# Attention heads of 64: values stationary, softmax weights moving and divided ahead of the turn

## The chip, the cores and the metric

The kernel runs on one core of a Trainium2 chip as one launch. The metric is the device time of one execution in microseconds. TensorE (PE in the profile) multiplies, VectorE (DVE) and ScalarE (ACT) work on tiles in SBUF and PSUM, GpSimd (POOL) helps, and SyncE (SP) issues the transfers.

## The reference, cut to what matters

The input is one sequence of 256 tokens with 1024 features. The reference runs two blocks of two layers, ten stages in the kernel: `pa` (pooling and attention), a convolutional feed-forward, a gated linear recurrence, a feed-forward, and then twice a hybrid attention layer (`hy0`, `hy1`), a feed-forward and a small gated embedding. All is fp32. What the change touches is attention:

```
pa:   8 heads of 64, causal, softmax over 256 keys
hy:   difference attention: 4 heads, 2 maps each, values of 128;  a = p[:, 0] - lam * p[:, 1]
      window attention:     8 heads of 64, 2 value heads;  p = e / (sum(e) + exp(sink - m))
      latent attention:     8 heads of 64 (96 in the scores)
      each: out = einsum('bhqk,bkhd->bqhd', p, v); the heads side by side go into a product with weights
```

## The kernel before, in words

Weights come as 241 units of 128x2048 fp32, in the order of use. For each unit SP brings it into one of three `raw` buffers, ACT rounds it to `w_hi` (`split`, L483), DVE forms `w_lo` (L990), and PE multiplies with three products (`three`, L1710 to L1712: high x high, high x low, low x high). A half unit is 24 such matmuls. A buffer of `w_hi` is free again once PE has used the unit three before (`w_used`).

Attention works on maps. A map is the 256x256 matrix of one head, or of one half of a difference head. `pa` has 8 maps. A hybrid layer has 24: maps 0 to 7 of the difference heads (width 128), 8 to 15 of the window heads (64, with a sink), 16 to 23 of the latent heads (64). Each engine has its own loop over maps, written out by hand:

- PE (`attention`, in the block of TensorE): at odd i, `scores(i+1)` computes maps i+1 and i+2 in banks 4 and 5 (L1972, on two halves of the rows at once). Then a filler: half a weight unit of gates. Then `outputs(i-1)` (L2019): per map four matmuls, with the turned softmax weights stationary and the values moving (64 or 128 columns), result by tokens. Then `transposed` for map i (L1991), and for some i also for a pair of finished output tiles, four transposes each.
- DVE (`attention` in the block of VectorE): per odd i it does `logits(i+1)` (L1245 to L1252: distance term, maximum, sink), the evacuation of the filler (L1067), `logits(i+2)`, at i=11 the scaling of the difference outputs, then `outputs` of a group that has ended (L1264 on: reciprocal of the sums, outputs times the reciprocal) and last the split of one weight unit.
- ACT (`attention` in the block of ScalarE): `turn(i-1)` copies the transposed map from its bank into `pt` (L674), `softmax(i)` takes the exponentials with their sums (L693, L695), and at odd i follows the split of a weight unit. For latent maps with odd i `softmax(i)` comes ahead of the turn. Pairs of turned outputs are copied by `turn` as well (L676, L679).

The semaphore `exp_done` releases the transposes of a map, `pt_done` the copy, `pt_ev` the output product, `pv_done` the group on DVE, `o_ev` the transposes of the pair. With a distance term `logits(i)` writes `lg[i % 2]`, so it waits for the transposes of map i-2. In `hy` the product of map 23 stands inside the first product with the branch weights (`onto`, L1710 on), which itself writes the banks that the outputs leave.

## Time and profile before

| | us |
|---|---|
| Median of 3 runs (1570.85 to 1575.32) | 1570.9 |
| The profiled execution | 1571.56 |
| Its span, first to last instruction | 1569.7 |
| PE busy | 1541.5 |
| DVE busy | 1144.7 |
| ACT busy | 910.6 |
| POOL busy | 156.7 |

The span is that of the instructions of the profiled execution; its own time lies 1.9 us above it. Lengths of PE's matmuls overlap, since they are pipelined, so the pace of PE is read from one start to the next and not from the lengths. One fp32 matmul shows as two records (two passes), a product of the kind `three` as one record for each of its three parts. The attention of `pa` lies at about 45 to 90 us, that of `hy0` at 670 to 800, that of `hy1` at 1160 to 1290, and the two hybrid ones repeat each other.

### The profile page before, as it was taken

The numbers are of one execution on the slowest core, as the hardware profiler recorded it, in microseconds if no ns is written. First come the engines' busy times: TensorE is split into PE (matmuls) and PEld (weight loads), VectorE is DVE, ScalarE is ACT, GpSimd is POOL, SyncE is SP. The second block draws the span as 40 slices with busy tenths as digits, with TensorE's granted clock in tenths as the row PEclk, the third lists the DMA queues.
The fourth block names the chain that finished last, engine by engine and source line by source line (L and its number), as shares of the span: only waits on it lengthen the run. The fifth ranks groups of instructions, "written<-read, shape, count | busy, mean of one in ns | idle before, by whom it ended". The sixth has DMA issues, their size and how long they took to land.

```text
span 1569.7 us, 30181 instructions
## 1 busy us (share of the span) xinstructions
PE 1541.5 (98%) x12792; PEld 1494.6 (95%) x12792; DVE 1144.7 (73%) x1382; ACT 910.6 (58%) x1213; POOL 156.7 (10%) x91
## 2 busy tenths in 40 slices
PE   7999999999999999999999999999999999999998
PEld 7899999999999999899899999999889899999998
DVE  6768777888988787778458875678778647776666
ACT  6566544698666565556465644456645555644444
POOL 0211211100011110000030100010000013011010
PEclk9999999999999999999999999999999999999999
DMA  9345555444546545423244555544542334455552
GB/s 317 126 146 184 198 191 181 164 167 150 180 166 214 187 161 200 150 97 119 85 165 162 188 190 185 188 162 162 183 140 91 120 99 160 173 200 202 176 187 77
DMA packets 38412, 258.73 MB, mean 165 GB/s; under 512 B 4768, under 2 KB 5408, under 8 KB 7840
## 3 DMA queue, kind: packets, MB, share of 16 engines
q1 hardware_dynamic: 37872, 255.33, 46.9%
q8 instruction: 83, 1.36, 0.3%
q10 hardware_dynamic: 432, 1.84, 0.3%
q14 instruction: 25, 0.20, 0.0%
HBM read 256.10 MB, written 1.05 MB: 164 GB/s over the span
## 4 chain that ended last, share of the span: by engine, by line
PE 79%; issue 8%; ACT 6%; DVE 5%; POOL 0%; DMA 0%; SPq 0%; POOLq 0%; ACTq 0%; DVEq 0%
PE bank L1710 24%; PE bank L1712 23%; PE bank L1711 23%; PE bank L2019 3%; PE bank L1972 3%; PE bank L1991 2%; ACT w_hi L483 2%; DVE w_lo L990 2%; PE bank L1942 1%; DVE h_lo L1005 1%; PE bank L1915 1%; ACT h_hi L503 1%; DVE qk L1106 1%; DVE x L1081 0%; POOL y_lo L1632 0%
## 5 line engine op out<-in xcount | busy, mean ns | idle before, releaser
L1710 PE MATMUL bank<-h_hi,w_hi 128*128 128x256 f32 x2640 | 751.9, 285 | 14.2 <-DVE h_lo L1005 9.4
L1711 PE MATMUL bank<-h_lo,w_hi 128*128 128x256 f32 x2640 | 742.0, 281 | 0.0
L1712 PE MATMUL bank<-h_hi,w_lo 128*128 128x256 f32 x2640 | 741.8, 281 | 0.0
L990 DVE TENSOR_TENSOR w_lo<-raw,w_hi 128x2048 fp32r<-128x2048 f32 x237 | 549.6, 2322 | 168.6 <-ACT w_hi L483 167.4
L483 ACT ACTIVATE w_hi<-raw 128x2048 fp32r<-128x2048 f32 x237 | 452.8, 1912 | 237.5 <-PE bank L1712 237.5
L1710 PEld LDWEIGHTS bank<-h_hi,w_hi 128*128 128x128 f32 x2640 | 497.7, 189 | 26.6 <-issue 20.9
L1712 PEld LDWEIGHTS bank<-h_hi,w_lo 128*128 128x128 f32 x2640 | 500.9, 190 | 0.0
L1711 PEld LDWEIGHTS bank<-h_lo,w_hi 128*128 128x128 f32 x2640 | 497.3, 188 | 0.3
L1710 PE MATMUL bank<-y_hi,w_hi 128*128 128x256 f32 x1040 | 294.4, 283 | 3.1 <-DVE y_lo L1447 1.4
L1712 PE MATMUL bank<-y_hi,w_lo 128*128 128x256 f32 x1040 | 291.6, 280 | 0.0
L1711 PE MATMUL bank<-y_lo,w_hi 128*128 128x256 f32 x1040 | 291.5, 280 | 0.0
L1710 PEld LDWEIGHTS bank<-y_hi,w_hi 128*128 128x128 f32 x1040 | 195.4, 188 | 6.1 <-ACT sq L641 1.6
L1712 PEld LDWEIGHTS bank<-y_hi,w_lo 128*128 128x128 f32 x1040 | 196.6, 189 | 0.0
L1711 PEld LDWEIGHTS bank<-y_lo,w_hi 128*128 128x128 f32 x1040 | 195.2, 188 | 0.1
L1632 POOL TENSOR_TENSOR y_lo<-qk,y_hi 128x512 fp32r<-128x512 f32 x52 | 109.3, 2101 | 801.4 <-ACT y_hi L602 707.9
L1106 DVE SCALAR_TENSOR_TENSOR qk<-bank,vec,qk 128x255 f32<-128x255 f32 (+1 forms) x264 | 114.9, 477 | 41.1 <-ACT qk L576 32.7
L1056 DVE TENSOR_TENSOR bank<-bank,rinv_t 128x512 f32<-128x512 f32 (+1 forms) x123 | 84.8, 690 | 34.6 <-PE bank L1712 33.7
L576 ACT ACTIVATE qk<-bank,vec 128x256 f32<-128x256 f32 x88 | 44.6, 557 | 104.9 <-DVE bank L1056 104.8
L602 ACT ACTIVATE y_hi<-qk 128x512 fp32r<-128x512 f32 x44 | 27.5, 624 | 62.4 <-PE bank L1712 59.3
L591 ACT ACTIVATE qk<-qk 128x512 f32<-128x512 f32 x44 | 27.8, 633 | 60.3 <-DVE qk L1106 59.9
L674 ACT ACTIVATE pt<-bank 128x512 f32<-128x512 f32 x56 | 33.0, 589 | 48.3 <-PE bank L1991 48.2
L2019 PE MATMUL bank<-val,pt 128*128 128x64 f32 (+1 forms) x448 | 57.0, 270 | 0.7 <-ACT pt L674 0.7
(227 smaller groups left out, 1339.7 us busy)
## 6 DMA issues: line engine op xcount, KB each, us to landing
raw<-W SPq DMA_DIRECT2D x237, 1024.0 KB, 4.8
raw<-W SPq DMA_DIRECT2D x4, 512.0 KB, 7.4
wide<-RW ACTq DMA_DIRECT2D x1, 1280.0 KB, 6.9
x<-XT SPq DMA_DIRECT2D x4, 256.0 KB, 6.6
OUT<-x SPq DMA_DIRECT2D x4, 256.0 KB, 2.0
wide<-CON SPq DMA_DIRECT2D x1, 768.0 KB, 9.7
val<-PE_T ACTq DMA_DIRECT2D x2, 256.0 KB, 2.7
vec<-VEC SPq DMA_DIRECT2D x1, 390.0 KB, 4.6
```

The source lines that it names most:

```text
L483: nc.scalar.activation(w_hi[:, n0 % NW], raw[:, n0 % NRAW], ACT.Copy).then_inc(sems["hi_done"], 1)
L576: ins = nc.scalar.activation(T[:, t], up[:, t * S:(t + 1) * S], ACT.Identity, bias=b, scale=w)
L674: nc.scalar.activation(pt[:, u[1] % 2], src, ACT.Copy).then_inc(sems["pt_ev"], 1)
L990: V.tensor_tensor(w_lo[:, n0 % NW], raw[:, n0 % NRAW], w_hi[:, n0 % NW].bitcast(F32), ALU.subtract)\
L1056: return V.tensor_tensor(z, z, rinv.unsqueeze(1).broadcast_to([P, w // S, S]), ALU.mult)\
L1106: return V.scalar_tensor_tensor(out=dst, in0=src, scalar=w, in1=dst, op0=ALU.mult, op1=ALU.add)
L1632: return G.tensor_tensor(dst, src, hi.bitcast(F32), ALU.subtract)
L1710: T.matmul(out, w[0], a[0], start=start, stop=False, **kw)
L1711: T.matmul(out, w[0], a[1], start=False, stop=False, **kw)
L1712: return T.matmul(out, w[1], a[0], start=False, stop=stop, **kw)
L1972: last = T.matmul(b[:, qt * S:(qt + 1) * S], qk[p:p + w, tq, qt * P:(qt + 1) * P], qk[p:p + w, tk], start=a == 0, stop=a == n - 1)
L2019: last = T.matmul(o, pt[:, i % 2, kt * S + qt * P:kt * S + qt * P + P], value(m["v"], kt), start=kt == 0, stop=kt == 1)
```

## The change

For maps of width 64 (all of `pa`, maps 8 to 23 of a hybrid layer):

- Output product: the values (64 columns) are stationary, and the turned weights move (256 columns). Two heads are done together (`output_pair`), one into partitions 0 to 63 and one into 64 to 127 of their banks, so the result is by features. It is issued at even i for maps i-2 and i-1.
- The result needs no turn. ACT copies it out of its bank (`leave`), at i=17 and i=21, and after the first sigmoid for the last group; in `pa` at i=5 and after the loop.
- The division by the sums can't be done on a result by features. DVE divides the exponentials of each map (`divide`: in `lg`, two multiplies by the reciprocal, ahead of it the sink's add), and `norm_done` releases the transposes instead of `exp_done`.
- The window heads are ordered so that a pair always has one head for each half of the partitions.
- The difference heads (width 128) and the turns of their two pairs stay as they were.

The diff, cut to its core:

```diff
@@ -365,7 +365,8 @@
                                 v=("diff", h), g=h, slot=m, w=128, sink=None, col=2 * h + m))
-            for h in (0, 4, 1, 5, 2, 6, 3, 7):
+            for h in (0, 5, 1, 4, 2, 7, 3, 6):
+
                 p = 64 * (h // 4)
@@ -391,7 +392,7 @@
-        TURNS = {"pa": {5: [0], 8: [1]}, "hy": {12: [0], 13: [1], 16: [2], 17: [3], 21: [4], 24: [5]}}
+        TURNS = {"pa": {}, "hy": {12: [0], 13: [1]}}
@@ -672,11 +678,16 @@
                     nc.scalar.activation(pt[:, u[1] % 2], src, ACT.Copy).then_inc(sems["pt_ev"], 1)
-                elif kind(s) == "hy" and u[1] < 2:
+                else:
                     nc.scalar.activation(ot_tiles(s, u[1]), src, ACT.Copy, scale=v_(f"g_dout{s[-1]}"))\
                         .then_inc(sems["pt_ev"], 1)
-                else:
-                    nc.scalar.activation(ot_tiles(s, u[1]), src, ACT.Copy).then_inc(sems["pt_ev"], 1)
+
+            def leave(s, g):
+
+                gg = total(s, "ogroups") + g
+                act.wait_ge(sems["pv_done"], gg + 1)
+                nc.scalar.activation(ot_tiles(s, g if kind(s) == "pa" else g - 2), bank[2 + gg % 2][:], ACT.Copy)\
+                    .then_inc(sems["o_ev"], 1)
@@ -699,7 +710,10 @@
                 ub = B[s]
-                act.wait_ge(sems["pt_ev"], use_no(s, ("pair", p)) + 1)
+                if p < 2:
+                    act.wait_ge(sems["pt_ev"], use_no(s, ("pair", p)) + 1)
+                else:
+                    act.wait_ge(sems["o_ev"], total(s, "opairs") + p + 1)
                 if p >= 2:
@@ -732,9 +746,14 @@
-                        turn(s, ("pair", 0))
-                        act.wait_ge(sems["pt_ev"], use_no(s, ("pair", 0)) + 1)
+                        leave(s, 0)
+                        act.wait_ge(sems["o_ev"], total(s, "opairs") + 1)
+
+                        act.wait_ge(sems["w_used"], B[s] + 8)
                         to_h(s, hf, 2)
+                    if kind(s) == "hy" and i in (17, 21):
+                        for g in {17: (4, 5), 21: (6,)}[i]:
+                            leave(s, g)
                     held = (9, n - 1) if kind(s) == "hy" else (5,)
@@ -761,6 +780,7 @@
+                leave(s, 1)
                 act.wait_ge(sems["vec_in"], 16)
@@ -770,8 +790,7 @@
                     to_h(s, hf, j)
-                turn(s, ("pair", 1))
-                act.wait_ge(sems["pt_ev"], use_no(s, ("pair", 1)) + 1)
+                act.wait_ge(sems["o_ev"], total(s, "opairs") + 2)
                 to_h(s, hf, 3)
@@ -911,10 +930,10 @@
                     nc.scalar.activation(g, g, ACT.Sigmoid).then_inc(sems["sig_done"], 1)
+                    if b == 0:
+                        leave(s, 7)
                     if b < 2:
                         branch_input(s, b + 2)
-                    if b == 0:
-                        turn(s, ("pair", 5))
                 branch_input(s, 4)
@@ -1252,30 +1271,27 @@
+            def divide(s, i):
+
+                m, a = att_maps(s)[i], 2 + i % 2
+                dve.wait_ge(sems["exp_done"], total(s, "maps") + i + 1)
+                z = sums[:, m["col"]]
+                if m["sink"] is not None:
+                    link(V.tensor_tensor(z, z, esink[:, m["sink"]], ALU.add))
+                link(V.reciprocal(rec[:, a], z))
+                for qt in range(2):
+                    p = lg[:, i % 2, qt * S:(qt + 1) * S]
+                    last = V.tensor_scalar(p, p, rec[:, a, qt:qt + 1], None, ALU.mult)
+                last.then_inc(sems["norm_done"], 1)
+
             def outputs(s, g):
-                K, ms = kind(s), att_maps(s)
+                ms = att_maps(s)
                 mine = sorted((m for m in ms if m["g"] == g), key=lambda m: m["col"])
                 a, n, gg = mine[0]["col"], len(mine), total(s, "ogroups") + g
                 dve.wait_ge(sems["pv_done"], gg + 1)
-                if mine[0]["sink"] is not None:
-                    h = mine[0]["sink"]
-                    link(V.tensor_tensor(sums[:, a:a + n], sums[:, a:a + n], esink[:, h:h + n], ALU.add))
                 link(V.reciprocal(rec[:, 0:n], sums[:, a:a + n]))
                 O = bank[2 + gg % 2]
-                pairs = total(s, "opairs")
-                if K == "pa" or g >= 4:
-                    p = g if K == "pa" else g - 2
-                    if p >= 2:
-
-                        dve.wait_ge(sems["pt_done"], use_no(s, ("pair", p - 2)) + 1)
-                    src = O[:].rearrange("p (q h d) -> p q h d", q=2, h=4)
-                    dst = ot[:, p % 2].rearrange("p (q h d) -> p q h d", q=2, h=4)
-                    for q in range(2):
-                        last = V.tensor_tensor(dst[:, q], src[:, q], rec[:, 0:4, q].unsqueeze(2).broadcast_to([P, 4, 64]),
-                                               ALU.mult)
-                    last.then_inc(sems["o_ev"], 1)
-                    return
                 h, L = g, hys.index(s)
@@ -1303,6 +1319,8 @@
                 logits(s, 1)
+                if kind(s) == "pa":
+                    divide(s, 0)
                 if kind(s) == "hy":
@@ -1318,6 +1336,8 @@
+                    if att_maps(s)[i]["w"] == 64 and att_maps(s)[i]["dist"]:
+                        divide(s, i)
                     if i + 1 < n:
@@ -1328,6 +1348,10 @@
                         logits(s, i + 2)
+                        if att_maps(s)[i + 1]["w"] == 64:
+                            divide(s, i + 1)
+                            if not att_maps(s)[i + 2]["dist"]:
+                                divide(s, i + 2)
                     if kind(s) == "hy" and i == 11:
@@ -1341,7 +1365,7 @@
                     for e in (i - 1, i):
-                        if ended(s, e) is not None:
+                        if ended(s, e) is not None and att_maps(s)[e]["w"] == 128:
                             outputs(s, ended(s, e))
@@ -1981,7 +2005,10 @@
                 if u[0] == "map":
-                    pe.wait_ge(sems["exp_done"], total(s, "maps") + u[1] + 1)
+                    if att_maps(s)[u[1]]["w"] == 64:
+                        pe.wait_ge(sems["norm_done"], normed_no(s, u[1]))
+                    else:
+                        pe.wait_ge(sems["exp_done"], total(s, "maps") + u[1] + 1)
                     src = lg[:, u[1] % 2]
@@ -1995,24 +2022,12 @@
                 m = att_maps(s)[i]
-                g = total(s, "ogroups") + m["g"]
-                if kind(s) == "pa" and i == 0:
-
-                    pe.wait_ge(sems["qk_done"], total(s, "pairs") + 4)
-                if kind(s) == "pa" and i == 4:
-
-                    pe.wait_ge(sems["in_ev"], total(s, "groups") + 7)
-                if kind(s) == "hy" and i == 0:
+                output_bank(s, i)
+                if i == 0:
                     pe.wait_ge(sems["in_ev"], total(s, "groups") + 18)
-                if m["slot"] == 0 and m["g"] >= 2:
-
-                    if kind(s) == "hy" and m["g"] - 2 < 4:
-                        pe.wait_ge(sems["od_free"], 4 * hys.index(s) + m["g"] - 1)
-                    else:
-                        pe.wait_ge(sems["o_ev"], total(s, "opairs") + m["g"] - 2 - 2 + 1)
                 pe.wait_ge(sems["pt_ev"], use_no(s, ("map", i)) + 1)
-                b = bank[2 + g % 2]
+                b = bank[2 + (total(s, "ogroups") + m["g"]) % 2]
                 for qt in range(2):
@@ -2020,6 +2035,37 @@
                     last.then_inc(sems["pv_done"], 1)
+
+            def output_bank(s, i):
+                m = att_maps(s)[i]
+                if m["g"] >= 2 and all(e["g"] != m["g"] for e in att_maps(s)[:i]):
+
+                    if m["g"] - 2 < 4:
+                        pe.wait_ge(sems["od_free"], 4 * hys.index(s) + m["g"] - 1)
+                    else:
+                        pe.wait_ge(sems["o_ev"], total(s, "opairs") + m["g"] - 2 - 2 + 1)
+
+            def output_pair(s, i):
+
+
+                if kind(s) == "pa" and i == 0:
+
+                    pe.wait_ge(sems["qk_done"], total(s, "pairs") + 4)
+                if kind(s) == "pa" and i == 4:
+
+                    pe.wait_ge(sems["in_ev"], total(s, "groups") + 7)
+                output_bank(s, i)
+                output_bank(s, i + 1)
+                pe.wait_ge(sems["pt_ev"], use_no(s, ("map", i + 1)) + 1)
+                for kt in range(2):
+                    for e in (i, i + 1):
+                        m = att_maps(s)[e]
+                        a, r = m["slot"] // 2, 64 * (m["slot"] % 2)
+                        last = T.matmul(bank[2 + (total(s, "ogroups") + m["g"]) % 2][r:r + 64, a * S:(a + 1) * S],
+                                        value(m["v"], kt), pt[:, e % 2, kt * S:(kt + 1) * S],
+                                        start=kt == 0, stop=kt == 1, skip_group_check=True)
+                        if kt and ended(s, e) is not None:
+                            last.then_inc(sems["pv_done"], 1)
@@ -2030,10 +2076,10 @@
                         fill(i)
-                    if kind(s) == "pa" and i == 5:
-                        transposed(s, ("pair", 0))
-                    if i and (kind(s) == "pa" or i < n):
+                    if i and att_maps(s)[i - 1]["w"] == 128:
                         outputs(s, i - 1)
+                    elif i and i % 2 == 0 and (kind(s) == "pa" or i < n):
+                        output_pair(s, i - 2)
                     if kind(s) == "hy" and i == 0:
@@ -2280,10 +2325,9 @@
                             onto(s, b, ub + 25, y_parts(0), True, False, between={
-                                2: lambda: outputs(s, 23),
+                                2: lambda: output_pair(s, 22),
                                 4: lambda: pe.wait_ge(sems["o_ev"], total(s, "opairs") + 5),
                                 6: lambda: pe.wait_ge(sems["o_ev"], total(s, "opairs") + 6)})
-                            transposed(s, ("pair", 5))
                         else:
```

## Rows read from the trace of the kernel before

**Rows 1.** Busy time of each engine, from the page.

```profile
PE 1541.5 (98%) x12792; PEld 1494.6 (95%) x12792; DVE 1144.7 (73%) x1382; ACT 910.6 (58%) x1213; POOL 156.7 (10%) x91
```

**Rows 2.** Busy by stretch: length, then PE, PEld, DVE, ACT, POOL, clock; `hy0`.

```profile
700.00:770.00 70.00, 70.00 (x583) 64.67 (x583) 49.84 (x83) 41.89 (x100) 0.00 (x0) 1.00 0.31 108
```

**Rows 3.** Order of time on PE, maps 8 and 9: start, length, engine, line.

```profile
716.92 0.60 PE L1991 MATMUL bank<-con,lg 128*128 128x128 f32 x4
717.45 1.14 PE L1972 MATMUL bank<-qk 64*128 64x256 f32 x8
718.52 0.39 PE L1710 MATMUL bank<-h_hi,w_hi 128*128 128x256 f32 x1
...
721.47 1.00 PE L2019 MATMUL bank<-val,pt 128*128 128x64 f32 x8
722.30 0.61 PE L1991 MATMUL bank<-con,lg 128*128 128x128 f32 x4
722.67 0.36 PE L1710 MATMUL bank<-h_hi,w_hi 128*128 128x256 f32 x1
```

**Rows 4.** Order of time on PE, a burst on column tiles in `pa`.

```profile
41.40 1.06 PE L1915 MATMUL bank<-sq,con 128*32 128x256 f32 x8
42.39 0.39 PE L1710 MATMUL bank<-w_hi,h_hi 128*128 128x256 f32 x1
```

**Rows 5.** Order of time on PE, map 12 and the turn of pair 0.

```profile
736.01 0.60 PE L1991 MATMUL bank<-con,lg 128*128 128x128 f32 x4
736.45 0.60 PE L1991 MATMUL bank<-con,ot 128*128 128x128 f32 x4
```

**Rows 6.** Order of time on DVE, a multiply in SBUF, and outputs with sink.

```profile
417.92 0.34 DVE L1190 TENSOR_SCALAR geo<-lg,small 128x256 f32<-128x256 f32 x1
...
753.82 0.16 DVE L1263 TENSOR_TENSOR sums<-sums,esink 128x8 f32<-128x8 f32 x1
...
754.25 0.76 DVE L1275 TENSOR_TENSOR ot<-bank,rec 128x256 f32<-128x256 f32 x2
```

**Rows 7.** Order of time on ACT, maps 7 to 9 of `hy0`.

```profile
712.11 1.91 ACT L483 ACTIVATE w_hi<-raw 128x2048 fp32r<-128x2048 f32 x1 [2.59 <-PE bank L1712]
...
715.67 0.19 ACT L695 ACTIVATION_READ_ACCUMULATOR lg<-lg,nm 128x1 f32 x1
717.56 0.60 ACT L674 ACTIVATE pt<-bank 128x512 f32<-128x512 f32 x1 [1.70 <-PE bank L1991]
```

**Rows 8.** Order of time on DVE, difference outputs and the split behind them.

```profile
715.03 0.17 DVE L1264 RECIPROCAL rec<-sums 128x4 f32<-128x4 f32 x1
...
717.78 0.17 DVE L1264 RECIPROCAL rec<-sums 128x4 f32<-128x4 f32 x1
...
720.52 2.28 DVE L990 TENSOR_TENSOR w_lo<-raw,w_hi 128x2048 fp32r<-128x2048 f32 x1
722.72 0.68 DVE L1245 SCALAR_TENSOR_TENSOR lg<-con,bank 128x512 f32<-128x512 f32 x1
```

**Rows 9.** Order of time on ACT, end of the exponentials of map 12.

```profile
734.86 0.19 ACT L695 ACTIVATION_READ_ACCUMULATOR lg<-lg,nm 128x1 f32 x1
```

**Rows 10.** Order of time on ACT and PE, map 22.

```profile
791.10 0.21 ACT L695 ACTIVATION_READ_ACCUMULATOR lg<-bank,nm 128x1 f32 x1
...
791.61 0.61 PE L1991 MATMUL bank<-con,lg 128*128 128x128 f32 x4
```

**Rows 11.** Order of time on PE and ACT, outputs of map 23, first sigmoid.

```profile
797.61 1.00 PE L2019 MATMUL bank<-val,pt 128*128 128x64 f32 x8
...
800.09 1.92 ACT L913 ACTIVATE wide<-wide 128x2048 f32<-128x2048 f32 x1
```

**Rows 12.** Order of time on PE, a gap elsewhere in the kernel.

```profile
401.65 0.70 PE L1780 MATMUL bank<-sq,con 128*128 128x256 f32 x2 [1.85 <-DVE sq L1043]
```

**Rows 13.** PE by stretch behind that gap: length, busy, count, granted clock, DMA.

```profile
402.40:405.70 3.30, 3.30 (x18) 0.50 0.49 149
```

**Rows 14.** Order of time on PE, outputs of map 7 in `pa`.

```profile
84.75 1.10 PE L2019 MATMUL bank<-val,pt 128*128 128x64 f32 x8 [0.69 <-ACT pt L674]
```

More of the change, by code:

```diff
@@ L189, in build @@
             cst_done crms cf_done chi c_ready rope_mm rope_done kro_done
-            s_done lp_done exp_done pt_done pt_ev pv_done o_ev od_free od_ss od_root
+            s_done lp_done exp_done norm_done pt_done pt_ev pv_done o_ev od_free od_ss od_root
             pool_p pm_done psc sig_done bhi b_ready
@@ L309, in build @@
         PLAN = {
-            "pa": dict(groups=8, parts=0, pairs=4, sets=2, maps=8, ogroups=2, opairs=2),
-            "hy": dict(groups=30, parts=5, pairs=13, sets=3, maps=24, ogroups=8, opairs=6)}
+            "pa": dict(groups=8, parts=0, pairs=4, sets=2, maps=8, ogroups=2, opairs=2, turned=0, scaled=8),
+            "hy": dict(groups=30, parts=5, pairs=13, sets=3, maps=24, ogroups=8, opairs=6, turned=2, scaled=16)}
         def total(s, what):
@@ L402, in use_no @@
         def use_no(s, what):
-            n = total(s, "maps") + total(s, "opairs")
+            n = total(s, "maps") + total(s, "turned")
             for i in range(PLAN[kind(s)]["maps"] + 1):
@@ L409, in use_no, with normed_no @@
                     n += 1
+        def normed_no(s, i):
+            if att_maps(s)[i]["w"] == 64:
+                return total(s, "scaled") + sum(m["w"] == 64 for m in att_maps(s)[:i]) + 1
         def ot_tiles(s, p):
@@ L2117, in pa @@
                 onto(s, 0, ub + 8, h_parts(2), True, False, part=(6, 7))
-                transposed(s, ("pair", 1))
                 for n, j in enumerate((0, 1, 3)):
```

## The prediction

> **What bounds the kernel now.** I read the page's busy shares first, to find the engine that sets the end, then the busy time by stretch for one hybrid attention, then the order of time on PE, VectorE (DVE) and ScalarE (ACT). The page gives PE 98% of the span [rows 1]. In the attention of the first hybrid layer PE is busy for the whole 70 us, DVE for 71% and ACT for 60% [rows 2]. So PE work that goes is time won, as long as the other two engines still deliver before PE arrives. DVE and ACT run in order: one late item holds all behind it, whatever their mean share. That is what I look for.
>
> One turn of the loop over maps on PE (odd map i, then i+1) reads in [rows 3]: transposes of map 8 at 716.92, scores at 717.45 (0.53 later), the half unit of weights of map 9 at 718.52, outputs of map 8 at 721.47 (2.95 later), transposes of map 9 at 722.30 (0.84 later), the next half unit at 722.67 (0.37). I call the times of PE "arrivals".
>
> **What PE saves.** Before, the outputs of one head cost 0.84 us although they have 64 columns [rows 3], so 1.68 for two heads. After, a pair is four matmuls of 256 columns with 64 stationary columns each, two side by side. The nearest row is a burst of the same count on tiles of 32 columns: from 41.40 to 42.39, 0.99 us for eight records (four matmuls in two passes) [rows 4]. Going into a tiled burst costs the group ahead 0.53 - 0.37 = 0.16 [rows 3]. So 1.15; I take 1.20, since 64 columns load slower than 32 (lower bound 0.99, upper bound by the scores of the same kind, 1.07 + 0.16 = 1.23, if the tiles do run together). A pair saves 0.48. There are 4 + 8 + 8 = 20 pairs: 9.6 us. The turn of a pair of output tiles goes in 2 + 4 + 4 = 10 places, 0.44 us each (736.01 to 736.45, of the same four transposes) [rows 5]: 4.4 us. The sum is 14.0 us: 2.8 in "pa", 5.6 in each hybrid layer.
>
> The Trainium skill, "TensorEngine Tiling (Array Packing)", section Key Properties, says that a change of tiling mode drains the array. It speaks against this change, which adds one such change in and out per pair. The trace agrees: eight records in 0.99 us plus 0.16 ahead, where records two by two at the spacing of 0.21 would be 0.86. Without that drain the pairs would save 0.82 each, 16.4 in all, rather than 9.6.
>
> **What the division costs DVE.** New per map: a reciprocal of 128x2 and two multiplies of 128x256 from SBUF to SBUF by a column; for windows also the sink's add. The add and reciprocal are 753.82 to 754.25, 0.43; one such multiply takes 0.34 [rows 6], so two in a row are at most 0.68, which gives 1.1 us with a sink and 0.9 without (lower bound 0.8, from two overlapped; upper bound 1.2, with the 0.76 that the old pair of multiplies takes). It is 16 maps a layer, some 16 us of DVE against some 4 removed. DVE goes from 50 to about 62 of 65 to 75 us: it still fits, on the mean. But PE's transposes now wait for it and it stands in DVE's order, so each is a possible stall. Layer by layer, place by place:
>
> - Map 8. The exponentials end at 715.86 [rows 7]; DVE divides to 717.0; PE arrives at 716.92. Stall 0.1.
> - Map 9, the large one. At odd i DVE divides map i as the first thing of its turn of the loop. For i=9 that lies behind everything of turn 7: the difference outputs of groups 2 and 3 (715.03 to 717.78 to 720.52, 2.74 each) and the split of a weight unit (720.52 to 722.72, 2.20) [rows 8]. Those now start after the division of map 8, at 717.0: done at 717.0 + 5.5 + 2.2 = 724.7, map 9 divided at 725.8. PE comes to these transposes after scores and a half unit, with no outputs before them any more: 717.6 + 1.07 + 2.95 = 721.6. Stall 4.2 us. The exponentials of map 9 are no part of it: the turn of map 8 starts at 717.56 [rows 7] and they follow it.
> - Maps 10, 12, 14. ACT's order is split, turn, exponentials; its split waits for the end of the odd half unit (712.11, for the 711.9 of PE) and the exponentials are done 3.75 after it starts [rows 7]. So their end is tied to PE, not to DVE. For map 12 they end at 735.05 [rows 9] and PE arrives at 736.01 [rows 5], 0.96 of slack. PE now arrives 0.48 earlier and the division takes 1.1: 0.48 + 1.1 - 0.96 = 0.6. With what queues behind the late map 9 I take 0.7 each, 2.1 in all.
> - Turn of pair 0 (map 12). The scaling of its tiles on DVE now stands behind the division of map 12: two small ones (0.43) and two multiplies (0.76, both by the [rows 6]), 1.1 to 1.2, less the 0.44 of the transposes of map 12: 0.7.
> - Maps 16, 18, 20: no sink, 0.1 each by the same sum: 0.3.
> - Map 22. Exponentials end at 791.31, PE arrives at 791.61 [rows 10]: slack 0.3. PE now arrives 0.48 + 0.44 earlier, the division adds 0.9, ACT has one copy less ahead (0.5): 0.92 + 0.9 - 0.3 - 0.5 = 1.0.
> - Last pair. Its bank is now emptied by ACT, behind a sigmoid that runs from 800.09 to 802.0 [rows 11], plus a copy of 0.6 [rows 7]: 802.6. Before, DVE did it. PE comes from 797.61 [rows 11] with 1.2 for the pair and 24 matmuls (2.9 at the pace of rows 3): 801.7. Stall 0.9.
>
> That is 0.1 + 4.2 + 2.1 + 0.7 + 0.3 + 1.0 + 0.9 = 9.3 us of stalls against 5.6 saved: each hybrid layer gets 3.7 longer.
>
> **The clock.** After a PE gap of 1.85 us (the matmul at 401.65) the granted clock is 0.50 of 2.4 GHz, so the 1.2 GHz level, over the next 3.3 us, with 18 matmuls where the pace of [rows 3] (24 in 2.95) would fit 27 [rows 12, 13]: about 1.1 us lost. A gap of 4.2 is longer; part of the loss falls into the stall of map 10. I take 0.8 per layer (bounds 0 and 1.7).
>
> The Trainium skill, "TensorE: Matmul & The Clock Gate", section Why this matters for your kernels, warns of idle gaps between bursts for this reason; the trace agrees for one gap, and no row shows one as long as 4 us.
>
> **"pa".** 2.8 saved. Added: a division (0.9) before the very first transposes, and another in the last chain, where PE already waits on the exponentials and their copy (84.75, idle 0.69) [rows 14]; and what follows waits for the split of the rows of h. I let 0.3 of the 2.8 survive (bounds 0 and 2.8).
>
> **The sum.** 2 x (3.7 + 0.8) - 0.3 = +8.7 us. The profiled execution took 1571.56 us (span 1569.7, and 1.9 around it), so 1580.3; it lies 0.7 over the median of the runs, 1570.9. I predict 1580.
>
> **Everything else.** The order of the window heads changes which rows of a bank they write, not the count. On ACT a copy from the bank replaces a copy from the turn. The splits of DVE get late by some 4 us, but their unit is used two turns of the loop (some 20 us) later, and the transfer behind it has more than that. Cover for both: the three weight buffers.
>
> **Rivals.**
> 1. Everything hides: DVE has 20 us free in these 70 [rows 2], so the division costs nothing and 14.0 is won: 1557.6. Against it: the order of DVE around map 9 is written out, and the 4.2 follows from it.
> 2. Only the queue around map 9 stalls (2 x 4.2), the rest is covered by slack: 1571.6 - 14.0 + 8.4 = 1566. For it: the slacks of 0.3 to 1.1 are small numbers, and each of my 0.7s hangs on the 0.48.
> 3. The tiles don't run side by side, so the change doesn't do what it says: 8 passes of 0.21 and 0.2 around them, 1.9 a pair, 0.7 more than I take; where PE would stall anyhow (5 of 8 pairs a layer) it costs nothing. 4 + 3 + 3 pairs: +7, 1587. Against it: the 0.99 of [rows 4] is for 8 records of 256 columns, too short for them one by one.
>
> **Chances.** Forecast 0.64 (1575 to 1586 by the bounds of burst, division and clock); rival 1 0.10; rival 2, or a mix of it with the forecast from 1563 to 1575, 0.18; rival 3 0.08. Within 0.3% (1566.2 to 1575.6; about what a measurement of this kernel can't tell from no change) lies most of rival 2: 0.14. Faster 0.15, slower 0.71. The range 1567 to 1588 leaves out rival 1, a part of rival 2 and a little above.
>
> **What would show it.** Pair bursts of about 1.0 us with two records at each start; PE idle 4 us before the transposes of map 9 in both hybrid layers, with DVE's division as releaser, and a clock of 0.50 behind it; 0.7 before maps 10, 12 and 14; about 1 before the second half of the first branch product, released by ACT's copy. The prediction is wrong if map 9 is not awaited (then rival 1 or 2), or if a pair takes 1.7 or more (rival 3).

## The result, and the profile after

The changed kernel takes 1584.4 us (median of 20 runs, 1573.2 to 1588.2), the kernel before in runs beside it 1573.9 (median of 20, 1570.9 to 1575.3): ratio 1.0061, 95% interval 1.0052 to 1.0070, so 0.6% slower. The profiled execution took 1582.2 us, span 1580.4, against 1571.6 and 1569.7.

Page of the changed kernel, busy time of each engine [rows 1]:

```profile
PE 1532.0 (97%) x12592; PEld 1467.7 (93%) x12592; DVE 1171.4 (74%) x1484; ACT 911.1 (58%) x1213; POOL 155.0 (10%) x91
```

PE has 200 records fewer and 9.5 us less to do; the span is 10.7 longer. So PE waits. Busy by stretch in `hy0`, 70 us of the same attention as in [rows 2], starting 7 us later:

```profile
707.00:777.00 70.00, 63.91 (x495) 55.09 (x496) 54.34 (x116) 39.33 (x94) 0.00 (x0) 0.98 0.29 93
```

PE is busy for 63.9 of 70 us, with 88 records fewer; DVE went from 49.8 to 54.3. The order of time on PE shows where it waits, maps 9 to 14 [rows 3, 5]:

```profile
726.26 1.14 PE L1996 MATMUL bank<-qk 64*128 64x256 f32 x8
...
734.32 0.63 PE L2018 MATMUL bank<-con,lg 128*128 128x128 f32 x4 [3.87 <-DVE lg L1284]
...
739.24 1.08 PE L2064 MATMUL bank<-pt,val 128*64 128x256 f32 x8
740.25 0.66 PE L2018 MATMUL bank<-con,lg 128*128 128x128 f32 x4
...
750.06 0.63 PE L2018 MATMUL bank<-con,lg 128*128 128x128 f32 x4 [0.74 <-DVE lg L1284]
751.17 0.63 PE L2018 MATMUL bank<-con,ot 128*128 128x128 f32 x4 [0.48 <-DVE ot L1364]
...
761.50 0.63 PE L2018 MATMUL bank<-con,lg 128*128 128x128 f32 x4 [0.89 <-DVE lg L1284]
```

A pair (line L2064, 739.24 to 740.25) takes 1.01 us for eight records, and in the trace they start two by two, 0.01 us apart: the tiles run side by side. Map 9 is awaited 3.87 us, and its releaser is the division (L1284). From the scores of map 10 (the L1996 row) to the transposes of map 12 it is 23.80 us; before, 717.45 to 736.01, 18.56 [rows 3, 5]. DVE's own order says why [rows 8]:

```profile
724.94 0.62 DVE L1284 TENSOR_SCALAR lg<-lg,rec 128x256 f32<-128x256 f32 x2
725.48 0.17 DVE L1293 RECIPROCAL rec<-sums 128x4 f32<-128x4 f32 x1
...
728.23 0.17 DVE L1293 RECIPROCAL rec<-sums 128x4 f32<-128x4 f32 x1
...
730.97 2.28 DVE L1009 TENSOR_TENSOR w_lo<-raw,w_hi 128x2048 fp32r<-128x2048 f32 x1
733.17 0.15 DVE L1280 TENSOR_TENSOR sums<-sums,esink 128x2 f32<-128x2 f32 x1
...
733.56 0.62 DVE L1284 TENSOR_SCALAR lg<-lg,rec 128x256 f32<-128x256 f32 x2
```

Map 8 is divided, then come the outputs of groups 2 and 3 and the split, and only then map 9. Behind the gap the clock stands at its lower level, 1.2 of 2.4 GHz [rows 13] (all engines: PE, PEld, DVE, ACT, POOL, then the granted clock):

```profile
735.10:738.40 3.30, 3.30 (x17) 3.30 (x17) 2.73 (x7) 3.27 (x9) 0.00 (x0) 0.50 0.68 283
```

What this costs can be read from the rows: from the transposes of map 9 (734.32) over half a weight unit to the pair (739.24) it is 4.92 us; before, the same work took 0.37 + 2.95 = 3.32 [rows 3]. So the low clock costs 1.6 us.

At the end of the stage, order of time on PE, then ACT [rows 10, 11]:

```profile
803.19 1.08 PE L2064 MATMUL bank<-pt,val 128*64 128x256 f32 x8 [0.39 <-ACT pt L680]
805.18 0.63 PE L2018 MATMUL bank<-con,lg 128*128 128x128 f32 x4 [0.91 <-DVE lg L1284]
...
809.47 0.36 PE L1734 MATMUL bank<-y_hi,w_hi 128*128 128x256 f32 x1 [0.39 <-issue]
...
814.65 0.57 ACT L689 ACTIVATE qk<-bank 128x512 f32<-128x512 f32 x1
```

In "pa", order of time on PE:

```profile
52.23 0.66 PE L2018 MATMUL bank<-con,lg 128*128 128x128 f32 x4 [0.82 <-DVE lg L1284]
...
62.39 0.63 PE L2018 MATMUL bank<-con,lg 128*128 128x128 f32 x4 [1.11 <-DVE lg L1284]
...
77.88 0.35 PE L1734 MATMUL bank<-h_hi,w_hi 128*128 128x256 f32 x1 [1.12 <-DVE wide L1086]
...
85.76 0.63 PE L2018 MATMUL bank<-con,lg 128*128 128x128 f32 x4 [1.78 <-DVE lg L1284]
```

The transposes of maps 0, 2 and 7 wait for their divisions, 3.7 us in all (map 4 another 0.17). Before, none of them waited, the place of the 1.12 had 0.84, and the 0.69 ahead of the last product stands in both kernels.

The table below gives stage lengths in every trace: the time between the same two matmuls of weight units, counted from the first, so that kernels can be laid beside each other. "pa" is up to the 481st, `hy0` from the 5041st to the 5761st, `hy1` from the 8641st to the 9121st, which ends ahead of the last pair; the loops are the three looped feed-forward stretches (720, 1680 and 1800 matmuls). "10 to 12" is the time from the scores of map 10 to the transposes of map 12 in `hy0`.

```
kernel                     pa    hy0    hy1    loops              10 to 12
before                     85.9  141.3  102.3  83.2 201.4 215.6   18.56
changed                    90.9  146.4  107.3  85.2 197.2 211.4   23.80
no_division                83.9  137.6   98.0  85.2 197.2 211.4   18.01
division_alone             90.4  149.4  110.4  85.2 201.4 215.6   23.48
pairs_hybrid               85.9  146.4  107.2  85.2 197.2 215.7   23.78
pairs_latent               85.4  142.5  103.3  85.2 201.4 211.4
pairs_latent_inputs_late   86.4  141.2  102.0  85.2 201.4 215.6
pairs_latent_scaled_first  86.3  140.0  100.8  85.2 201.4 215.6
nine_early                 86.9  147.9  108.8  85.2 201.4 215.6   25.21
nine_early_split_late      87.4  143.3  104.1  85.2 201.4 215.6   20.64
root_late                  87.1  147.6  105.3  85.2 201.4 215.6   23.38
pool_left_out              85.7  147.3  107.1  85.2 201.4 211.4
before_again               86.1  141.3  102.3  85.2 201.4 215.6
changed_again              89.9  146.4  107.3  83.2 201.4 215.6
```

So by stage the change costs 5.0 in "pa", 5.1 in `hy0` and 5.0 in `hy1`; the loops, whose code it doesn't touch, gave 6.4 back in this one execution, and 1.6 went in a stretch ahead of `hy0` where the clock was low.

The profiled execution is not a typical one. The mean granted clock of the 20 runs lies between 0.993 and 0.997, in 13 of them at 0.996 or more; the profiled one has 0.993, the lowest value. As an estimate, 0.993 means 2 x 0.007 x 1580 = 22 us at the lower level and 0.996 means 13. The stretches behind map 9 take 6.8 of these in both layers together and the end of the kernel 2.3, so in most runs there was hardly room for the 6.8 us of low clock that this trace shows in "pa" (below). The loss of 5.0 there overstates what most runs lose.

### The profile page after: what moved, and what is told of

It is laid out like the page before. It is cut to its first block, busy times and chain, and to the rows that moved or that the text cites. A ratio compares the mean times of both kernels' runs of the same rounds, so it can differ in the third digit from the quotient of the medians.

```text
span 1580.4 us, 29864 instructions
## 1 busy us (share of the span) xinstructions
PE 1532.0 (97%) x12592; PEld 1467.7 (93%) x12592; DVE 1171.4 (74%) x1484; ACT 911.1 (58%) x1213; POOL 155.0 (10%) x91
## 4 chain that ended last, share of the span: by engine, by line
PE 74%; ACT 9%; issue 9%; DVE 7%; POOL 0%; DMA 0%; ACTq 0%; SPq 0%; POOLq 0%; DVEq 0%
PE bank L1734 23%; PE bank L1736 22%; PE bank L1735 22%; ACT w_hi L489 3%; PE bank L1996 2%; DVE w_lo L1009 2%; PE bank L2018 1%; ACT lg L706 1%; PE bank L2064 1%; PE bank L2034 1%; DVE h_lo L1024 1%; DVE lg L1284 1%; PE bank L1939 1%; PE bank L1966 1%; ACT h_hi L509 1%
## 5 line engine op out<-in xcount | busy, mean ns | idle before, releaser
L608 ACT ACTIVATE y_hi<-qk 128x512 fp32r<-128x512 f32 x44 | 27.4, 624 | 59.7 <-PE bank L1736 54.3
L1656 POOL TENSOR_TENSOR y_lo<-hf,y_hi 128x512 fp32r<-128x512 f32 x8 | 16.7, 2098 | 369.7 <-ACT y_hi L721 369.7
```

What stands on the lines that cost most here:

```text
L1656: return G.tensor_tensor(dst, src, hi.bitcast(F32), ALU.subtract)
```

## The experiments

### The saving alone and the division alone

`no_division` leaves out DVE's division (outputs are not normalised); `division_alone` is the kernel before with the division added, so values are divided twice.

```diff
  # no_division
-                 divide(s, ...)                  (all four places)
-                     pe.wait_ge(sems["norm_done"], normed_no(s, u[1]))
+                     pe.wait_ge(sems["exp_done"], total(s, "maps") + u[1] + 1)
  # division_alone: before, and the same places and waits added
+                 divide(s, ...)
+                     pe.wait_ge(sems["norm_done"], normed_no(s, u[1]))
```

> The changed kernel without the division: VectorE's add of the sink, reciprocal and multiplies by the reciprocals are left out, and TensorE's transposes wait for the exponentials (so the outputs of these heads are not normalised). If TensorE's part of the change is worth what I counted and the stalls come from the division: 14.0 us saved over 20 pairs and 10 turns, some 2 given back at the ends: 0.992 of before, about 1561 us; no gap over 0.5 us before the transposes of map 9. If the pairs save little: 0.998 to 1.0. If something other than the division makes the changed kernel longer: above 1.0.

> The kernel before with the division added at the places where the changed kernel has it, the old product, scaling and turns kept (values are divided twice, so outputs are not the reference's). If the division's places in VectorE's order cost what I worked out: map 9 waits 3.5 us and loses 1 to the clock, map 22 0.6, the turn of pair 0 0.7, in each hybrid layer, and the first stage some 4 (it lost 4.3 in the changed kernel in spite of 2.8 saved, so up to 7): +15 to +20 us, ratio 1.010 to 1.013. If the division hides: below 1.002.

`no_division`: 0.9934 (0.9913 to 0.9955), 1562.6 us. `division_alone`: 1.0121 (1.0096 to 1.0146), 1594.9 us. Both ratios are as expected. The stages show 10.0 us saved without the division (2.0 + 3.7 + 4.3), and 4.5 + 8.1 + 8.1 = 20.7 lost by the division alone. The price of one pair can be read from a turn of the loop over latent maps, from one group of scores to the next, first in the kernel before, then without the division:

```profile
769.75 2.60 PE L1972 MATMUL bank<-qk 64*128 64x256 f32 x16
780.74 2.60 PE L1972 MATMUL bank<-qk 64*128 64x256 f32 x16
```

```profile
756.39 2.60 PE L1988 MATMUL bank<-qk 64*128 64x256 f32 x16
766.86 2.60 PE L1988 MATMUL bank<-qk 64*128 64x256 f32 x16
```

10.99 and 10.47: a pair saves 0.52 (I had taken 0.48). With 0.44 for each turn that would be 14.8 over the kernel; a third of it is lost even with no division. The idle time of PE that is new in its three attention stages adds up to 3.4 us of that: PE now comes early to other things. The rest was not placed. One of the new waits, in `hy0`:

```profile
726.42 0.63 PE L2008 MATMUL bank<-con,lg 128*128 128x128 f32 x4 [0.51 <-ACT lg L706]
```

### Which stage pays

`pairs_hybrid` has "pa" as before; `pairs_latent` has "pa" and the window maps as before.

```diff
+ PAIRED = ("mla", "win")        # pairs_latent: ("mla",)
- if att_maps(s)[i]["w"] == 64:  (division, waits, order of the maps, emptying of the banks)
+ if att_maps(s)[i]["v"][0] in PAIRED:
```

> The changed kernel with the first attention stage (8 causal maps) as before; window and latent maps of both hybrid layers by pairs. If the first stage costs 4 us of the change's 9 to 10: 1.003 of before and no displacement up to 100 us of the span. If the first stage is neutral, as I predicted (-0.3): 1.006, as the changed kernel.

> Only the 8 latent maps of each hybrid layer by pairs, all else as before. Saved per layer 4 pairs x 0.48 and 2 turns x 0.44 = 2.8; stalls 3 x 0.17 and 1.5 at map 22: -0.8 a layer, -1.6 us in all, ratio 0.999. If the division of these maps, which have no sink and stand late in VectorE's order, hid altogether: -5.6 us, 0.9965. If they stalled like the window maps (0.7 to 1 each): +2, 1.001.

`pairs_hybrid`: 1.0042 (1.0025 to 1.0059), "pa" 85.9 as before, both hybrid stages as in the changed kernel: so "pa" has its own share of the loss (1.0042 against 1.0061), and my forecast for it was wrong. `pairs_latent`: 0.9996 (0.9978 to 1.0014), which can't be told from 0.999 or from no change. By stage it was 1.2 and 1.0 longer than before, where I had expected 0.8 shorter. Two stalls at map 22 were the known ones; one was new (order of time on PE):

```profile
761.91 0.63 PE L2060 MATMUL bank<-con,ot 128*128 128x128 f32 x4 [1.00 <-DVE ot L1332]
```

The turn of pair 2 waits for the scaling of its tiles, which DVE now does behind the divisions of maps 16 and 17.

### GpSimd beside the division

`pool_left_out` is the changed kernel without the pooling branch's arithmetic on GpSimd (POOL).

```diff
-                     link(G.tensor_tensor(nxt[...], cur[...], cur[...], ALU.add))
-                         link(G.tensor_tensor(r, r, pa_con[...], ALU.mult))
-                         last = G.tensor_tensor(pool_u[...], r, pool_u[...], ALU.subtract)
+                     last = G.tensor_tensor(pool_u[:, g, 8:12], ...)     (4 columns)
```

> The changed kernel with GpSimd's adds and multiplies of the pooling branch in the first stage left out (the pooling branch is then not computed). If VectorE's multiplies of the division, up to 1.2 us instead of 0.35, are long because GpSimd works in SBUF at the same time, and the end of the stage waits for GpSimd: no multiply over 0.4 us there, the stage ends 3 us earlier than in the changed kernel (2 behind before instead of 5), 1.004. If they are long for another reason: they stay, the stage ends at most 1 us earlier, 1.006.

In the changed kernel, order of time on DVE and POOL in "pa":

```profile
60.71 1.53 DVE L1284 TENSOR_SCALAR lg<-lg,rec 128x256 f32<-128x256 f32 x2
62.16 2.81 DVE L1009 TENSOR_TENSOR w_lo<-raw,w_hi 128x2048 fp32r<-128x2048 f32 x1
...
70.83 0.62 DVE L1284 TENSOR_SCALAR lg<-lg,rec 128x256 f32<-128x256 f32 x2
...
79.20 1.86 DVE L1284 TENSOR_SCALAR lg<-lg,rec 128x256 f32<-128x256 f32 x2
...
84.39 1.22 DVE L1284 TENSOR_SCALAR lg<-lg,rec 128x256 f32<-128x256 f32 x2
```

```profile
62.05 0.77 POOL L1688 TENSOR_TENSOR wide<-wide 128x256 f32<-128x256 f32 x1
62.90 2.67 POOL L1689 TENSOR_TENSOR wide<-wide 128x256 f32<-128x256 f32 x1
77.14 6.73 POOL L1684 TENSOR_TENSOR wide<-wide 128x512 f32<-128x512 f32 x4 [11.57 <-DVE wide L1086]
```

The same two multiplies take 0.62 when POOL is idle and 0.90 to 1.86 (four of the eight pairs) when it works. Nor is it DVE alone that waits: DVE's split at 80.99 kept its 2.28 us, and POOL's last add, begun at 81.00, took 2.87 us, where the same add at 59.87 took 0.61:

```profile
81.00 2.87 POOL L1684 TENSOR_TENSOR wide<-wide 128x256 f32<-128x256 f32 x1
```

With POOL's work left out:

```profile
59.54 0.61 DVE L1284 TENSOR_SCALAR lg<-lg,rec 128x256 f32<-128x256 f32 x2
...
77.13 0.62 DVE L1284 TENSOR_SCALAR lg<-lg,rec 128x256 f32<-128x256 f32 x2
...
82.34 0.61 DVE L1284 TENSOR_SCALAR lg<-lg,rec 128x256 f32<-128x256 f32 x2
```

All eight pairs are at 0.61 or 0.62, and "pa" is 85.7 us long, not 90.9. Order of time on PE, maps 2 and 7:

```profile
60.30 0.63 PE L2010 MATMUL bank<-con,lg 128*128 128x128 f32 x4 [0.19 <-DVE lg L1284]
...
83.10 0.63 PE L2010 MATMUL bank<-con,lg 128*128 128x128 f32 x4 [1.18 <-DVE lg L1284]
```

The wait for map 2 fell from 1.11 to 0.19 and that for map 7 from 1.78 to 1.18, 1.5 us together. Three later kernels with the changed kernel's "pa" (`nine_early`, `nine_early_split_late`, `root_late`) split the loss: there the clock stayed at 1.00 and "pa" took 86.9 to 87.4. So about 1.4 us (87.1 - 85.7) is the contention with POOL, in line with the 1.5 of the two waits and half of the 3 that I had expected, and the other 3 to 4 are a low clock, which the changed kernel's trace shows as the last figures but two of this stretch of PE (length, busy, clock):

```profile
86.50:93.30 6.80, 6.22 (x20) 0.50 0.13 55
```

A low clock came here in both executions of the changed kernel (6.8 us of it in the first, about half in the second) and in `division_alone`, not in those three, though PE's gaps ahead were the same (1.78 and 0.69 us in the changed kernel, 1.77 and 0.69 in `nine_early`). What decides it stays open. The whole time of `pool_left_out`, 1.0065 (1.0041 to 1.0090), shows nothing of the gain: its trace has one loop at the longer 201.4 and lost 3.1 us to a low clock ahead of `hy0`. By the whole time alone this experiment is inconclusive; the verdict rests on the rows.

The Trainium skill, "SBUF — State Buffer", section SBUF: two separate sides, says that VectorE and GpSimd share a pair of ports, given to one of them for a whole instruction. The rows agree for the multiplies from SBUF to SBUF (0.90 to 1.86 for 0.62) and for POOL's add beside the split (2.87 for 0.61). I did not weigh it in the prediction.

### The order of DVE around map 9

```diff
  # nine_early: divide(9) between the outputs of groups 2 and 3
-                         divide(s, i)            (first of turn 9)
                              outputs(s, ended(s, e))
+                             if e == 6:
+                                 divide(s, 9)
  # nine_early_split_late: and the split of turn 7 behind divide(10)
-                         after(fillers[7][0])    (end of turn 7)
                              divide(s, i + 1)
+                             if i == 9: after(fillers[7][0])
  # root_late: and ScalarE's square root two maps later
-                     if kind(s) == "hy" and i == 9:
+                     if kind(s) == "hy" and i == 11:
```

> The changed kernel with VectorE's division of map 9 between the outputs of groups 2 and 3, not behind both and a split. By my theory the gap of 4.2 us before map 9 goes (divided at 729.4 in the time of the changed kernel's trace, TensorE there at 730.2) and most of it comes back one map later, for the logits of map 10 start no earlier than before: a gap of 3 to 4 us before the transposes of map 10; 1 us a layer gained: 1.005 of before. By the rival (only the place of map 9's division costs): 4 to 5 us a layer, 1.000.

> The same, and the split of the weight unit (2.2 us) moved from behind the outputs of group 3 to behind the division of map 10. By my theory map 10 then waits about 2.3 us and map 11 about 1: 2.2 to 3.2 us a layer gained against the changed kernel: 1.002 to 1.003 of before. By the rival, everything gained already by the place of map 9: 1.000, as the kernel beside it.

> As nine_early_split_late, and ScalarE's square root of the difference norms (it waits for the outputs of group 3, and the copy of the turned map 9 stands behind it) moved two maps later. If that copy alone held the pair of maps 8 and 9 (2.55 us in the kernel without this move): the gap before the pair goes and 2 us a layer are gained, 1.002 of before. If VectorE is the limit there, which is what I expect from its order (map 10 is divided at 731.8 in that trace, whatever ScalarE does): the gap moves to the transposes of map 10, at most 0.5 us a layer gained, 1.004 to 1.005.

`nine_early`: 1.0092 (1.0072 to 1.0112); `nine_early_split_late`: 1.0049 (1.0033 to 1.0065); `root_late`: 1.0070 (1.0057 to 1.0084). Order of time on PE in `nine_early`, map 10, and its clock behind it:

```profile
733.48 1.08 PE L2020 MATMUL bank<-con,lg 128*128 128x128 f32 x4 [4.38 <-DVE lg L1284]
```

```profile
733.50:740.00 6.50, 6.50 (x31) 0.56 0.45 159
```

Map 9 is not awaited any more, map 10 is, for 4.38 us: DVE starts its logits no earlier than before. That is my theory's sign, but not its price: I expected 1 us a layer gained, and 1.5 was lost, for the low clock lasted longer than behind the gap of 3.87 (0.50 from 732.3 to 739.1, against 3.4 us). With the split moved as well, order of time on PE, then by stretch:

```profile
731.95 0.63 PE L2022 MATMUL bank<-con,lg 128*128 128x128 f32 x4 [2.17 <-DVE lg L1284]
737.28 0.63 PE L2022 MATMUL bank<-con,lg 128*128 128x128 f32 x4 [0.59 <-DVE lg L1284]
```

```profile
732.00:737.50 5.50, 4.91 (x38) 1.00 0.45 147
```

2.17 at map 10 and 0.59 at map 11 (2.3 and 1 expected), no loss of clock, and both stages 3.1 to 3.2 shorter than in the changed kernel. The whole time shows less of it: 1.0049, where I had 1.002 to 1.003. The profiled run is again a favourable one, with a mean clock of 0.998; 7 of the 12 runs have 0.994 to 0.996, so their clock fell for longer, where isn't known.

`root_late` answers a question that I had put wrongly: the gap stood before the transposes of map 10 all along, not before the pair. It stayed there (2.19), as it must if DVE is the limit; but the moved square root has its own table, the exponentials' table is loaded again ahead of map 12 (1.28 us at 740.00), and a gap of 2.16 came there (1.38 in `hy1`). Order of time on PE in `hy0`, and its clock behind both gaps:

```profile
731.22 0.63 PE L2022 MATMUL bank<-con,lg 128*128 128x128 f32 x4 [2.19 <-DVE lg L1284]
...
743.94 0.63 PE L2022 MATMUL bank<-con,lg 128*128 128x128 f32 x4 [2.16 <-DVE lg L1284]
```

```profile
732.50:735.70 3.20, 3.20 (x15) 0.50 0.46 97
746.20:749.40 3.20, 3.20 (x16) 0.50 0.27 38
```

Here the clock fell behind gaps as long as the one behind which it had stayed at 1.00. That makes `hy0` 4.3 us longer than in `nine_early_split_late`; `hy1`, where the clock held, is 1.2 longer. So the move costs some 1.2 us a layer, and most of the 4.3 is clock.

### A version that might beat both

```diff
  # pairs_latent_inputs_late: pairs_latent, and on ScalarE
-                     if kind(s) == "hy" and i == n - 2:   (ahead of softmax(22))
+                     if kind(s) == "hy" and i == n - 1:   (behind softmax(23))
                          branch_input(s, 0)
                          branch_input(s, 1)
  # pairs_latent_scaled_first: and on VectorE
+                         if kind(s) == "hy" and i == 15:
+                             outputs(s, 4)
                          if by_pair(s, i + 1):
                              divide(s, i + 1)
```

> Only the latent maps by pairs, and ScalarE's two copies of the first branch inputs (2 x 0.52 us) moved from ahead of the exponentials of map 22 to behind those of map 23. If the gap of 1.3 to 1.5 us at map 22 comes from ScalarE's order: it falls to 0.5 or less, 1 us a layer, so -2 to -4 us against before, ratio 0.998. If that gap comes from VectorE (the divisions of maps 22 and 23 one behind the other): it stays, ratio 0.9996 as without the move. If the first branch product then waits for its inputs: above 1.000.

> As pairs_latent_inputs_late, and VectorE scales the outputs of window group 4 ahead of the divisions of maps 16 and 17, not behind them. The gap of 1.2 us before the turn of pair 2 falls to 0.5 or less, 0.8 us a layer: 0.998 of before (between 0.997 and 0.999). If the divisions behind it now make map 16 wait instead: no gain, 0.999.

0.9990 (0.9979 to 1.0001) and 0.9991 (0.9982 to 1.0001). The first move took 1.3 us off each layer against `pairs_latent` and both gaps at map 22 are gone; since `pairs_latent` had been 1 us a layer behind the kernel before, that makes 0.1 and 0.3 us against before, not the 1 to 2 of my 0.998. The second took another 1.2; the turn of pair 2 starts at once:

```profile
761.95 0.60 PE L2061 MATMUL bank<-con,ot 128*128 128x128 f32 x4
```

By stage this version is 2.8 us shorter than before in the hybrid layers. In whole times the gain is a tenth of a per cent and its interval includes 1, so it is no proven win.

### Two more executions

> The kernel before, a second profiled execution. If the two paces of the looped stages (115.6 or 118.3 ns from one matmul to the next) belong to an execution and not to a kernel: at least one of the three loops has another pace than in the first trace (83.2, 201.4, 215.6 us), and the time differs by 2 to 4 us for that alone. If they belong to the kernel: the same three numbers.

> The changed kernel, a second profiled execution. The stalls of the attention stages come again within 0.3 us (first stage 90.9 us, hybrid 102.3 and 54.5); the loops (85.2, 197.2, 211.4 us) may each come at the other pace if this belongs to an execution, and are the same if it belongs to the kernel.

`before_again` took 1574.9 us, `changed_again` 1589.2. The attention stages of both came again to 0.1 us in the hybrid layers (in "pa" 0.2 and 1.0 apart). The loops did not: PE by stretch (length, busy and records, clock), in the kernel before, the changed kernel, and the changed kernel again:

```profile
900.00:950.00 50.00, 50.00 (x425) 1.00 0.53 181
```

```profile
900.00:950.00 50.00, 50.00 (x435) 1.00 0.58 198
```

```profile
900.00:950.00 50.00, 50.00 (x425) 1.00 0.59 195
```

PE is fully busy at the full clock in all three, yet one did 435 matmuls and the others 425. The pace belongs to an execution, not to a kernel.

## Why the prediction was right, and where it was not

The forecast was 1580, the runs gave 1584; the sign, and the cause in the hybrid layers (DVE's order around map 9), were right. Two terms were not: "pa", which has the wrong sign, and the clock, which costs twice what I took. Term by term:

- Side by side: 1.01 a pair, as expected, so rival 3 falls. The saving is 0.52 a pair, not 0.48. Rival 1 falls too: the division doesn't hide, and even without it (1562.6) the 1557.6 isn't reached, for the old products had in part been cover for work of other engines.
- Map 9: 4.2 forecast, 3.87 idle in the row, and 4.15 from start to start. Clock behind it: 0.8 forecast, 1.6 found (inside my bounds of 0 and 1.7). Rival 2 (only map 9) falls, for maps 12 and 14, the turn of pair 0 and map 22 wait too.
- Maps 12 and 14: 0.7 each forecast, 0.74 and 0.89 idle. Map 10: 0.7 forecast, nothing found, since PE came to it 1.6 late at the low clock; so clock and map 10 together come to the 1.5 that I had, by two errors that cancel. Pair 0's turn: 0.7 and 0.48. Maps 16 to 20: 0.1 each and 0.17. Map 22: 1.0, found 0.91 before its transposes and 0.39 before the pair of maps 20 and 21.
- Last pair: 0.9 forecast, 0.26 found (PE's matmul at 815.28 comes 0.38 behind the one ahead, for 0.12 elsewhere); its copy stood behind the sigmoid as I said, but PE came later. In its place came 0.39 before the branch product, which I did not see.
- One hybrid layer: 3.7 + 0.8 = 4.5 forecast, 5.1 and 5.0 found. The pieces found, less 5.9 saved, make 4.4; 0.7 was not placed.
- "pa": this is the step that failed. I let 0.3 us of gain survive and set the bounds at 0 and 2.8, so no loss at all; found were 5.0 and 4.0 lost in the two traces, 1.0 to 1.5 where the clock held. The waits for divisions come to 3.9 us and the evacuation adds 0.3, against 3.0 saved (4 pairs at 0.52, two turns at 0.44): 1.2 lost. I named two added waits and did not price them place by place, as I had for the hybrid layers; map 2 I did not see at all. And I took the multiply from a row where POOL was idle: without POOL's work (`pool_left_out`) "pa" is 0.2 shorter than in the kernel before, which has that work; that is nearly my 0.3. The rest, up to 3.8, is the low clock, for which I had no term in "pa".

In the two pairs of traces the stages lose 14 to 15 us, yet the medians differ by 10.5. Taking for "pa" what it loses at full clock, 1.2, the stages lose 11.3, close to the medians, and the clock record of the runs (above) speaks for that; how often "pa" fell to the low clock was not counted. The sum of 8.7 is low by 1.8 against the medians: its errors, 1.5 in "pa" and 1.1 in the two layers, are small beside 10.5, but that the clock and map 10 cancelled is luck. The pace of the loops can move an execution by up to 10 us; whether the changed kernel gets the faster pace more often was not settled with two profiled executions of each.

## What to carry to other kernels

Work that one engine loses may have been the cover for another engine's chain: price an added wait by where it stands in the waiting engine's written order, not by the mean busy share. When a late item is moved forward in an engine that is full, ask what stands behind it: here the gap only moved one map on, until something with slack (the split) was moved out of the way, and of 3.87 us still 2.17 and 0.59 were left. Take the price of an added instruction from a row where the engines beside it are as busy as they will be. Give the small stage the same place-by-place sum as the large one. And before a profile is read as the kernel's time, compare its mean clock with that of the other runs.

## What the runs showed of the hardware

- Two paces of matmuls at full clock: 425 or 435 in 50 us (one start each 118.3 or 115.6 ns), fixed for a whole loop, changing from execution to execution; worth 2.0, 4.2 and 4.2 us in the three loops. What sets them stays open.
- Two DVE multiplies of 128x256 in SBUF: 0.62 us alone, 0.90 to 1.86 beside POOL. DVE's split: 2.28 alone, 2.81 in one place beside POOL; in another it kept 2.28, and POOL's add took 2.87 for 0.61.
- The clock. Behind gaps of 3.87 and 4.38 us it stood at 0.50 for some 3.4 and 5.7 us. Gaps of 2.16 to 2.19 us stand in `nine_early_split_late` (one in each hybrid layer) and in `root_late` (two in `hy0`, one in `hy1`): it fell behind two of the five, those in `hy0` of `root_late`, and stayed at 1.00 behind the others. In "pa" it fell in both traces of the changed kernel and held in `nine_early`, with the same gaps of 1.8 and 0.7. And in 7 of the 14 traces it fell ahead of `hy0` (at 660 to 667 us), where PE was never idle. So the length of a gap alone doesn't tell what the clock will do, and one trace doesn't settle it for a kernel.
